# FFN's first pair: gate and up chunks in turns by halves of the tokens, and an earlier seed in the first seven-product chunk

## The reference

```
h = rms_norm(x, ffn_norm)                       # x: 512 x 1024, after the mixer's residual
x = x + (silu(h @ w_gate) * (h @ w_up)) @ w_down   # w_gate, w_up: 1024 x 2816; w_down: 2816 x 1024
```

## Time and profile before

| what | value |
|---|---|
| median of 3 runs | 760.38 us |
| the profiled execution | 760.82 us, of which its span is 759.0 us |
| PE busy | 751.5 us (99%), 4542 matmuls |
| DVE busy | 591.5 us (78%) |
| ACT busy | 404.8 us (53%) |
| chain that ended last | PE 91%, DVE 3%, issue 2%, ACT 1%, DMA 1%, POOL 1% |

### The profile page before, as it was taken

One profiled execution on the slowest core, in us unless ns is written; L12 is line 12 of the kernel. 1 busy time (PEld: TensorE's weight loads), 2 busy tenths in 40 slices (PEclk: granted clock), 3 DMA queues, 4 the chain that ended last, 5 costly groups with the idle time before them and its releaser, 6 DMA issues.

```text
span 759.0 us, 11534 instructions
## 1 busy us (share of the span) xinstructions
PE 751.5 (99%) x4542; PEld 664.0 (87%) x4542; DVE 591.5 (78%) x816; ACT 404.8 (53%) x603; POOL 104.6 (14%) x130
## 2 busy tenths in 40 slices
PE   8999999999999999999999999999999999999998
PEld 8988888988888888888888799999888999999886
DVE  5636989878788966425978799889988888888991
ACT  6645546456663554545348565565544556565530
POOL 7100040457203221221230000000000000000000
DMA  8362223221133123317236444336073333339202
GB/s 270 103 194 68 93 62 112 67 101 55 56 112 110 57 59 110 111 55 276 85 94 173 122 167 122 113 108 242 1 250 111 112 112 112 111 112 313 75 28 83
DMA packets 67876, 89.54 MB, mean 118 GB/s; under 512 B 3108, under 2 KB 52592, under 8 KB 67696
## 3 DMA queue, kind: packets, MB, share of 16 engines
q1 hardware_dynamic: 66224, 85.60, 34.6%
q0 software_dynamic: 1456, 3.09, 2.0%
q10 hardware_dynamic: 144, 0.13, 0.1%
HBM read 81.99 MB, written 4.19 MB: 114 GB/s over the span
## 4 chain that ended last, share of the span: by engine, by line
PE 91%; DVE 3%; issue 2%; ACT 1%; DMA 1%; POOL 1%; DVEq 0%; POOLq 0%; SPq 0%
PE bank L2305 14%; PE bank L2307 14%; PE bank L2306 14%; PE bank L2743 8%; PE bank L2745 8%; PE bank L2744 8%; PE bank L2804 5%; PE bank L2808 5%; PE bank L2806 5%; PE bank L2686 1%; PE bank L2685 1%; PE bank L2684 1%; DMA w_lo<-plain 1%; PE bank L2394 1%; PE bank L2563 1%
## 5 line engine op out<-in xcount | busy, mean ns | idle before, releaser
L2305 PE MATMUL bank<-h_hi,w_hi 128*128 128x512 f32 (+1 forms) x352 | 134.6, 383 | 0.2 <-DVE w_lo L1557 0.2
L2307 PE MATMUL bank<-h_hi,w_lo 128*128 128x512 f32 (+1 forms) x352 | 133.7, 380 | 0.0
L2306 PE MATMUL bank<-h_lo,w_hi 128*128 128x512 f32 (+1 forms) x352 | 133.6, 380 | 0.0
L1485 DVE TENSOR_TENSOR w_lo<-raw,w_hi 128x2048 fp32r<-128x2048 f32 x31 | 73.4, 2369 | 41.3 <-ACT w_hi L873 33.3
L2743 PE MATMUL bank<-t_hi,w_hi 128*128 128x256 f32 x320 | 88.5, 276 | 0.4 <-ACT w_hi L1312 0.4
L2744 PE MATMUL bank<-t_lo,w_hi 128*128 128x256 f32 x320 | 88.3, 276 | 0.0
L2745 PE MATMUL bank<-t_hi,w_lo 128*128 128x256 f32 x320 | 88.3, 276 | 0.0
L2305 PEld LDWEIGHTS bank<-h_hi,w_hi 128*128 128x128 f32 x352 | 66.2, 188 | 12.6 <-ACT w_hi L936 0.4
L2307 PEld LDWEIGHTS bank<-h_hi,w_lo 128*128 128x128 f32 x352 | 66.2, 188 | 12.6
L2306 PEld LDWEIGHTS bank<-h_lo,w_hi 128*128 128x128 f32 x352 | 66.2, 188 | 12.1
L2743 PE MATMUL bank<-f_hi,w_hi 128*128 128x256 f32 x240 | 66.3, 276 | 0.0
(11 more groups left out here) (349 smaller groups left out, 1841.4 us busy)
## 6 DMA issues: line engine op xcount, KB each, us to landing
raw<-in_w_in_dram SPq DMA_DIRECT2D x26, 1024.0 KB, 5.1
raw<-in_w_ffn_up_dram SPq DMA_DIRECT2D x11, 1024.0 KB, 5.1
raw<-in_w_ffn_gate_dram SPq DMA_DIRECT2D x10, 1024.0 KB, 5.1
raw<-in_w_ffn_down_dram SPq DMA_DIRECT2D x7, 1024.0 KB, 5.0
raw<-in_w_branch_dram SPq DMA_DIRECT2D x4, 1024.0 KB, 4.9
b<-in_w_ffn_down_dram SPq DMA_DIRECT2D x4, 1024.0 KB, 6.4
x_sb<-in_x_dram SPq DMA_DIRECT2D x6, 512.0 KB, 4.7
o<-in_w_out_dram SPq DMA_DIRECT2D x3, 1024.0 KB, 9.8
```

The costliest lines, as they stand in the source:

```text
L1485: vec.tensor_tensor(w_lo[:, at], raw[:, c % 2, 0:n], w_hi[:, high].bitcast(F32), ALU.subtract)\
L2305: mm(dst, l_hi, r_hi, start=start, stop=False)
L2306: mm(dst, l_hi, r_lo, start=False, stop=False)
L2307: return mm(dst, l_lo, r_hi, start=False, stop=stop)
```

## The change

1. The first pair runs in four parts: gate half 0, up half 0, gate half 1, up half 1, all with 256 columns (`plain_part`). The up chunk has 96 matmuls of 256 columns in place of 48 of 512. The transposes of tiles 2 and 3 move into up half 0. The gate's results go to banks 2 and 3, so that it waits for eight `out_add` only; the up chunk uses the other two and waits for all ten.
2. The up weights are prepared as the gate weights are: ACT writes `p1_hi` and minus the whole into `p1_lo` (new buffers), a second accumulating DMA from POOL adds the whole. DVE's `split(PLAIN[1])` and ACT's are gone.
3. ACT's squares and copies stand in another order, with one buffer for the squares' output; on DVE the last `out_add` stands ahead of the variance of tile 2.
4. In the first seven-product chunk DVE makes two of the four weight sums, then the seed, then the other two sums. S1 x T1 waits for three low parts of T, A22 x T4 for the fourth.

```
-            for half in range(2):
-                cols = slice(half * SEQ // 2, (half + 1) * SEQ // 2)
-                pe.wait_ge(S["h2_lo_ready"], TT * (half + 1) - 1)
-                for j in range(CT):
-                    b = take_bank(fill_at[first] + j)
-                    pe.wait_ge(S["x1_taken"], (9, OUT_ADDS)[j])
...
-                        if (half, j, k) == (0, 1, 0):
-                            turn_h2(2)
-                        elif (half, j, k) == (0, 1, 2):
-                            turn_h2(3)
...
-            rows_chunk(first + 1, CW, up_bank, f_hi, f_lo)
+            def plain_part(up, half):
+
+                c = PLAIN[up]
...
+                pe.wait_ge(hi_ready, c + 1)
+                pe.wait_ge(lo_ready, c + 1)
                 pe.wait_ge(S["h2_lo_ready"], TT * (half + 1) - 1)
+                pe.wait_ge(S["x1_taken"], (8, OUT_ADDS)[up])
                 for j in range(CT):
+                    b = bank[(fill_at[c] + j) % 2] if up else bank[2 + j]
...
+                        if up and half == 0 and k == 0:
+                            turn_h2(2 + j)
                     if half == 1:
                         last.then_inc(filled, 1)
+            for half in range(2):
+                for up in range(2):
+                    plain_part(up, half)
```

```
@@ GpSimd @@
+            for n, (low, whole) in enumerate(((w_lo[:, at:at + CHUNK], plain0[:, :]), (p1_lo[:, :], raw[:, PLAIN[1] % 2, :]))):
+                pool.wait_ge(S["out_seeded"], 7 + n)
+                if n:
+                    pool.wait_ge(S["plain_added"], 16)
+                pool.dma_start(low, whole, accum_op=ALU.add).then_inc(S["plain_added"], 16)
@@ VectorE, the loop over WINO @@
-                sums_ahead(c + 1)
+                if m == 0:
+                    weight_sums(c + 1, (0,))
+                else:
+                    sums_ahead(c + 1)
...
                 vec.tensor_tensor(f1[:, T1ST], first[:, T1ST], seventh[:, up, :], ALU.add).then_inc(S["c21_seeded"], 1)
                 if m == 0:
+                    weight_sums(c + 1, (1,))
@@ TensorE, wino_chunk @@
-                pe.wait_ge(S["t_lo_ready"], 4)
+                pe.wait_ge(S["t_lo_ready"], 3)
                 product(one[:, T1ST], S1, T1, False)
...
+                pe.wait_ge(S["t_lo_ready"], 4)
                 product(f1[:, T1ST], A22, T4, False)
```

More of the change, by code:

```diff
@@ L1252, in square @@
                 act.wait_ge(S["x1_taken"], added)
-                if n >= 2:
-                    act.wait_ge(S["squares_summed"], 4 + n - 1)
+                if n:
+                    act.wait_ge(S["squares_summed"], 4 + n)
                 late = TT * (half == (1 if t < 2 else 0))
-                nact.activation(two[:, n % 2, :], x_sb[:, t, half * HALF:(half + 1) * HALF], ACT.Square,
+                nact.activation(two[:, 1, :], x_sb[:, t, half * HALF:(half + 1) * HALF], ACT.Square,
                                 accum_out=sums[:, late + t:late + t + 1]).then_inc(S["squares_summed"], 1)
@@ L1297, in _ @@
             act.wait_ge(S["out_tile"], len(OUT_ORDER))
-            split(PLAIN[1])
             def wino_split(c, step):
@@ L1386, in _ @@
                 act.wait_ge(filled, fill_at[PLAIN[0]] + j + 1)
-                gated(0, j, bank[(fill_at[PLAIN[0]] + j) % 2])
+                gated(0, j, bank[2 + j])
             split_ahead(WINO[0], 0, 1)
@@ L2008, in _ @@
             h2_low(1)
+            out_add(6, 1, 3, 0, 8)
             variance(2, 7)
@@ L2705, in _ @@
                             pe.wait_ge(S["h2_lo_ready"], TT * (half + 1))
-                        w = slice(w_at(first) + k * CW + j * P, w_at(first) + k * CW + (j + 1) * P)
-                        high = slice(w.start + hi_pad(first), w.stop + hi_pad(first))
-                        last = three(b[:, cols], w_hi[:, high], w_lo[:, w], f_hi[:, k, cols], f_lo[:, k, cols],
-                                     k == 0, k == KT - 1)
-                        if (half, j, k) == (0, 1, 0):
-                            turn_h2(2)
-                        elif (half, j, k) == (0, 1, 2):
-                            turn_h2(3)
+                        w = slice(k * CW + j * P, k * CW + (j + 1) * P)
+                        begin, end = k == 0 and half == 0, k == KT - 1
+                        mm(b[:, cols], c_hi[:, w], f_hi[:, k, cols], start=begin, stop=False, skip_group_check=True)
+                        mm(b[:, cols], c_hi[:, w], f_lo[:, k, cols], start=False, stop=False, skip_group_check=True)
+                        last = mm(b[:, cols], c_lo[:, w], f_hi[:, k, cols], start=False, stop=end, skip_group_check=True)
+                        if up and half == 0 and k == 0:
+                            turn_h2(2 + j)
                     if half == 1:
                         last.then_inc(filled, 1)
-            pe.wait_ge(hi_ready, first + 2)
-            pe.wait_ge(lo_ready, first + 2)
-            def up_bank(j):
-                pe.wait_ge(S["gate_taken"], j + 1)
-                return bank[(fill_at[first + 1] + j) % 2]
-            rows_chunk(first + 1, CW, up_bank, f_hi, f_lo)
+            for half in range(2):
+                for up in range(2):
+                    plain_part(up, half)
             B11, B21, B22 = (LOWER, T1ST), (UPPER, T1ST), (UPPER, T2ND)
```

47 lines of the change are left out of this document (28 added, 19 removed).

## The result

After takes 764.87 us (median of 6 runs, 763.02 to 766.67), before 760.83 us (6 runs, 760.29 to 761.24). The ratio is 1.0052, 95% interval [1.0038, 1.0066]. The forecast was 760.4 us with a range of 759.4 to 761.2 and a chance of 0.08 for slower by more than 0.2%. It was wrong, in sign and in range.

A forecast was written before the change was run, and what follows sets the result against it. DVE's chain, not PE, sets when S1 x T1 starts; PE's 0.28 + 0.71 + 1.29 us are waited away, the seed's 0.81 us goes to `c12` (0.74) and restart (0.1): 0.0 us, so 760.4 us, range 759.4 to 761.2.

The forecast's parts named there:

- The up weights: Low up weights for up half 0: transfer issued about 423.8, data there 6.9 us later at 430.7, needed at 434.8.
- only helps: SP's load of the next chunk: starts at about 423 in place of 426.25, taken as no harm.
- POOL has nothing else queued: Issue of the up weights' accumulating transfer: POOL issues 0.3 us after ACT's copies end at about 423.5.
- The rival for this: Second accumulating transfer comes late for up half 0, from 11 us between issue and landing: 762.8 us; chance 6%.
- PE through the first pair: Gate and up chunks: PE's pauses of 0.28, 0.71 and 1.29 us go; seven products can begin 2.5 us earlier.
- 0 to 0.28: Bounds in us on the gain from PE's pause ahead of the gate chunk, taken as gone in full.
- More matmuls, no more columns: Up chunk: 96 matmuls of 0.1136 us for 48 of 0.2273 us, 10.91 us either way, cost 0.
- What is late next: Gate complete 3 us later, so DVE's first weight sum waits until 447.6, against 447.09; the 2.3 us saved are waited away.
- The earlier seed: Seed behind two sums instead of four: PE starts S1 x T1 at 460.57 against 461.38, 0.81 us earlier.
- It stands some 2 us: PE's pause ahead of S1 x T1: PE itself would be there at 458.4 but goes at 460.57.
- What waits for the two sums: ACT's `c12` comes late for S4 x B22, at 464.16 against PE's own 463.4; 0.07 us of 0.81 left.
- The sum: Whole change: PE's early gains waited away, seed's 0.81 us less 0.74 us and 0.1 us restart: 0.0 us.

The follow-up runs named there:

- `fill_both`: The changed kernel with 18 extra unused matmuls ahead of up half 0 and 14 ahead of S1 x T1; 763.52 us, ratio 1.0036.
- `load_waits`: The changed kernel with the first seven-product chunk's load issued only after the second accumulating transfer has landed; 762.31 us, ratio 1.0014.
- `c12_first`: The changed kernel with DVE making the up weights' low part, 14 unused matmuls ahead of S1 x T1, ACT's `c12` ahead of two `hidden_high`; 760.55 us, ratio 0.9998.
- `waits_fill`: The changed kernel with the load issued after the second accumulating transfer and 14 unused matmuls ahead of S1 x T1; 761.26 us, ratio 1.0005.
- `seed_c12`: The kernel before with part 4 of the change alone, plus ACT's `c12` moved ahead of `hidden_high`; 760.13 us, ratio 0.9990.
- `fill`: The changed kernel with 14 unused matmuls in the pause ahead of S1 x T1; 765.54 us, ratio 1.0063.

## Why the prediction was wrong, point by point

**The step that failed is "The up weights".** It took the second accumulating transfer at 6.9 us from the earlier trace rows, issued at 423.8, landing at 430.7 against a need at 434.8, and said of the load beside it that an earlier start "only helps". Measured were 427.18, 11.0 us and 438.2. Two errors are in it, and it took both. The 6.9 us is the duration of a transfer beside which little ran: in before the up load's last 2.0 us (it landed at 421.3) and then nothing. After the change the second transfer runs beside a load of 1 MB from start to end, because both wait for the first transfer; the load does not start at 423, as the forecast had it, but at 426.72. And the issue is late: the first transfer takes 9.7 us, which the forecast's "POOL has nothing else queued" passed over, and ScalarE waits for the up load in this execution. Up half 0 could have started at 436.2. A transfer of 11.0 us issued at 423.8, or one of 8.0 us issued at 427.18, would have been in time. The rival for this was there, with its point of decision at 11 us and a time of 762.8 us; `fill_both` shows 763.5 us for it. It had the sharing right but not the late issue. It was given 6%, on the ground that the queue had 4 us to spare; 3.4 us of them went to the issue alone.

**"PE through the first pair": right but for one condition.** The 0.71 us and the 1.29 us went away as worked out, and so did the 0.28 us ahead of the gate in 12 of 14 profiles. In after's own they grew to 0.45 us. The bound "0 to 0.28" left out the loss side: ScalarE's copies of the up weights now stand ahead of the squares, and where the up load lands late (9.5 and 9.7 us) everything behind it slips. The load took 9.9 us in before too; there nobody waited for it, so the row of waits did not show it, and the forecast did not ask when it lands.

**"More matmuls, no more columns": right.** The up chunk's 96 matmuls keep the step of 0.11 us, and the runs without the late transfer are level with before.

**"What is late next" and "The earlier seed": right.** DVE was idle until the gate was complete; 12.29 us to the seed and 0.68 us to PE are exact, and about 2 us of pause came. Both the pause and its place had been forecast. What had not been is what the pause does to the matmuls behind it.

**The missing term: the clock.** "It stands some 2 us" was booked as time that had been won before and was only waited away. In before the longest pause here was 1.29 us, and the stretch from 429 to 438 us had a granted clock of 1.00. After has two of about 2 us, and behind one of them PE ran at 1.2 GHz until 468.0. It costs 1.6 us there, and the clock was below 0.999 in five of six executions. Neither a term nor a rival had it. That a pause of 2 us brings it on is shown by filling; where between 1.29 and 2 us it begins was not tried.

**"What waits for the two sums": right in kind, somewhat large.** After's profile hides it, because the slow matmuls give `c12` time. In `load_waits` the pause ahead of S4 x B22 is 0.50 us by starts, put down to `c12`; 0.76 us were forecast (the sum has 0.68 us for the two `hidden_high`, where the earlier trace rows give 0.76 us; in `load_waits` it was 0.61 us from their start to `c12`). `c12_first` takes it away by the order on ACT.

**The sum.** With the late transfer and the pauses' effect taken away, `waits_fill` is at 1.0005 [0.9996, 1.0013], the forecast's zero. The sum was right for the parts that it had; it lacked 2.3 to 2.8 us for the transfer and 1.4 us in the median for the clock. How the 0.9 us ahead of the changed part come about is open; at that place the other profiles scatter from 428.3 to 429.3.

## What to carry to other kernels

A transfer's duration read from a trace holds for what ran beside it there: when a change moves or adds one, list the transfers whose intervals now overlap and price those as sharing, look for transfers that wait for the same event (they always meet), and follow who is issued behind them. When a change makes an engine need a load earlier, read when that load lands; the waits of the old kernel do not show it. Swapping several short pauses of TensorE for one long one is not neutral even if the sum of idle time stays: look at the granted clock in windows right behind each pause, since busy times hide it, and test with a few matmuls without use in the pause. And when a suppliers' chain sets the end, work that is closed up ahead of it only makes a pause longer; the small reordering of who is served first (`seed_c12`) was the only part that showed a gain, of 0.6 us.

## What the runs showed of the hardware

- An accumulating transfer of 1 MB from SBUF to SBUF took 6.9 us in before, beside the last 2.0 us of a load. The second one of the changed kernel took 7.6 to 8.0 us with the load put off (four profiles) and 10.9 to 12.1 us beside a 1 MB load from HBM (seven profiles); that load took 6.0 to 6.9 us, against 5.1 us in before. The Trainium skill (DMA: Bandwidth & Descriptors, section on queues, rings and completion order) states that each engine serves its queues in turn, a packet at a time; these times agree with such sharing, but no run here isolates it.
- Behind pauses of 1.9 to 2.1 us in an otherwise unbroken stream, and behind one of 3.4 us, the granted clock fell to the 1.2 GHz level in some executions for 3 to 4 us; in others of the same kernel, with such a pause (2.40 us in the profile of `fill`), it did not. The step of a matmul of 256 columns went from 0.1136 to 0.213 us.
- 48 more weight loads with half as many columns behind each cost nothing that shows: the step is 0.1136 us for 256 columns with a new load each.
- GpSimd's `tensor_tensor` on 128x512 took 2.2 us each, and doubled a DVE row with both inputs in SBUF from 1.21 to 2.30 us.
